# Twelve modulation units of a two-block transformer kernel, moved from GpSimd to TensorE

## What is computed

```python
mod_x = jax.nn.silu(c) @ ada_w[l] + ada_b[l]
sh1, sc1, g1, sh2, sc2, g2 = jnp.split(mod_x[:, None, :], 6, axis=-1)
hx = modulate(rmsnorm(x, norm1_g[l]), sh1, sc1)
...
att_x = latent_attention(qx, jnp.concatenate([kx, kc], axis=1), jnp.concatenate([vx, vc], axis=1))
y_x = merge_branches(fourier_mix(fx), att_x, gx, w_fourier[l], w_mla_o[l], b_gate[l], w_out[l])
x = x + g1 * y_x
h2 = modulate(rmsnorm(x, norm2_g[l]), sh2, sc2)
x = x + g2 * sq_relu_mlp(h2, w_up[l], w_down[l])
```

## Time and profile before

| | |
|---|---|
| median of 3 runs | 2260.36 us (2259.75 to 2266.12) |
| profiled execution | 2260.59 us |
| its span, first to last instruction | 2258.6 us |
| busy: PE, DVE, ACT, POOL | 2176.6, 888.0, 840.9, 880.4 us |
| mean granted TensorE clock | 0.987 |

### The profile page before, as it was taken

The page is one execution under the profiler, slowest core; times in us unless marked ns, Lnnn a source line. Parts: engine busy times, 40 slices in busy tenths (PEclk is TensorE's granted clock), DMA queues, the critical chain, the costliest instruction groups (busy, mean ns, idle before and its releaser), DMA issues.

```text
span 2258.6 us, 28704 instructions
## 1 busy us (share of the span) xinstructions
PE 2176.6 (96%) x11528; PEld 1807.7 (80%) x11528; DVE 888.0 (39%) x1391; ACT 840.9 (37%) x1263; POOL 880.4 (39%) x640
## 2 busy tenths in 40 slices
PE   6999999989999989999999999999999999999998
PEld 3776678868888867989888888787888988888887
DVE  2357955441211246585666210505144243222102
ACT  3456542232322335253543423636233443223212
POOL 0334964434445434031221344041354624444441
PEclk9999989999999999999999999999999999999998
DMA  6411334423232233020211122222233412233221
GB/s 227 161 56 57 114 122 131 156 71 104 97 94 93 94 114 98 20 75 19 94 38 38 56 94 94 76 75 75 75 112 93 150 38 94 93 105 99 93 93 56
DMA packets 179969, 205.89 MB, mean 91 GB/s; under 512 B 3365, under 2 KB 170769, under 8 KB 179473
## 3 DMA queue, kind: packets, MB, share of 16 engines
q1 hardware_dynamic: 176912, 195.17, 26.7%
q10 hardware_dynamic: 2944, 9.15, 1.1%
HBM read 198.01 MB, written 6.29 MB: 90 GB/s over the span
## 4 chain that ended last, share of the span: by engine, by line
PE 81%; POOL 6%; DVE 4%; ACT 2%; issue 1%; DMA 0%; ACTq 0%; DVEq 0%; SPq 0%; POOLq 0%
PE ps L2092 21%; PE ps L2094 21%; PE ps L2093 21%; PE ps L2192 3%; POOL w_lo L692 2%; PE ps L2623 2%; POOL raw L709 2%; PE ps L2636 2%; POOL raw L711 2%; PE ps L2713 2%; PE ps L2730 1%; ACT w_hi L764 1%; PE ps L2139 1%; PE ps L2141 1%; PE ps L2140 1%
## 5 line engine op out<-in xcount | busy, mean ns | idle before, releaser
L692 POOL TENSOR_TENSOR w_lo<-raw,w_hi 128x512 fp32r<-128x512 f32 x586 | 777.2, 1358 | 1313.7 <-ACT w_hi L764 1313.6
L2092 PE MATMUL ps<-h_hi,w_hi 128*128 128x512 f32 x1384 | 558.0, 403 | 14.3 <-DVE h_lo L1427 4.9
L2094 PE MATMUL ps<-h_hi,w_lo 128*128 128x512 f32 x1384 | 542.0, 392 | 0.0
L2093 PE MATMUL ps<-h_lo,w_hi 128*128 128x512 f32 x1384 | 541.3, 391 | 0.0
L764 ACT ACTIVATE w_hi<-raw 128x2048 fp32r<-128x2048 f32 x150 | 285.7, 1904 | 366.2 <-PE ps L2094 359.5
L2092 PEld LDWEIGHTS ps<-h_hi,w_hi 128*128 128x128 f32 x1384 | 261.5, 189 | 75.2 <-issue 10.7
L2094 PEld LDWEIGHTS ps<-h_hi,w_lo 128*128 128x128 f32 x1384 | 261.2, 189 | 56.0
L2093 PEld LDWEIGHTS ps<-h_lo,w_hi 128*128 128x128 f32 x1384 | 262.0, 189 | 52.1 <-issue 1.2
L2092 PE MATMUL ps<-g_hi,w_hi 128*128 128x512 f32 x256 | 99.7, 389 | 0.0
L2094 PE MATMUL ps<-g_hi,w_lo 128*128 128x512 f32 x256 | 99.6, 389 | 0.0
L2093 PE MATMUL ps<-g_lo,w_hi 128*128 128x512 f32 x256 | 99.6, 389 | 0.0
(11 more groups left out here) (422 smaller groups left out, 3815.7 us busy)
## 6 DMA issues: line engine op xcount, KB each, us to landing
raw<-w_in SPq DMA_DIRECT2D x48, 1024.0 KB, 5.2
raw<-w_down SPq DMA_DIRECT2D x27, 1024.0 KB, 5.0
raw<-ada_w SPq DMA_DIRECT2D x24, 1024.0 KB, 5.2
raw<-w_gate_up SPq DMA_DIRECT2D x22, 1024.0 KB, 5.1
raw<-w_up SPq DMA_DIRECT2D x16, 1024.0 KB, 5.4
raw<-w_mkv SPq DMA_DIRECT2D x8, 1024.0 KB, 5.3
raw<-w_out SPq DMA_DIRECT2D x4, 1024.0 KB, 5.3
xT<-bias_band SPq DMA_DIRECT2D x2, 2048.0 KB, 9.8
```

What stands on the lines that cost most here:

```text
L692: ins = nc.gpsimd.tensor_tensor(w_lo[:, split_at[u] % 2, cols], raw[:, u % 2, cols], w_hi[:, split_at[u] % 2, cols].bitcast(F32), ALU.subt ...
L2092: T.matmul(out_, wh, hi, start=start, stop=False, skip_group_check=True)
L2093: T.matmul(out_, wh, lo, start=False, stop=False, skip_group_check=True)
L2094: return T.matmul(out_, wl, hi, start=False, stop=stop, skip_group_check=True)
```

## The change

GpSimd's `modulate` and the two batches in the attention go. The 12 units are multiplied on TensorE, one ahead of the transposes of each even item from 2 to 24 (`ROWS_AT`): the row tiles k = 0 to 3 go to the four column groups of 32 (PSUM partitions 0, 32, 64 and 96), k = 4 to 7 are added to them, with `silu_wide`, 32 columns for each k of which only the first isn't zero. The products lie in the free half of bank 5, so ScalarE's copy of that item takes 1024 columns instead of 768 and brings them into `probT1`. Behind the scores of item 2a + 6 (`PICKED_AT`) TensorE multiplies both halves of unit a's copy by the constant `pick` (1 at partitions 0, 32, 64 and 96), two matmuls of one column, and VectorE adds `ada_b` between its maximum and the scaling of it. VectorE fills `silu_wide` behind item 0. The loads keep their order; a slot is free when the rows are multiplied (`ada_mm`) and not when GpSimd is done. The batch of four in the MLP stays.

The diff, without the list of semaphore names, the value of `pick` and one raised count:

```diff
 CONST_AT, CONST_N = {}, 0
-for _name, _cols in [("ident", P), ("ones", P), ("tri", P), ("incl", P)]:
+for _name, _cols in [("ident", P), ("ones", P), ("tri", P), ("incl", P), ("pick", 1)]:
...
     prob1 = r("prob1", [P, 2, S + C])
-    probT1 = r("probT1", [P, 2, S + C])
-    ada_sum = r("ada_sum", [P, 8, 256])
+    probT1 = r("probT1", [P, 2, S + C + 256])
+    silu_wide = r("silu_wide", [P, KT, 32])
+    ada_sum = r.over("ada_sum", [P, 4, 256], BASE + 92 * 1024)
...
     BY_VECTOR = [12, 13, 14, 15]
-    BY_POOL = [a for a in range(16) if a not in BY_VECTOR]
-    BATCH = [range(0, 10), range(10, 12), range(12, 16)]
+    ROWS_AT = {2 * a + 2: a for a in range(12)}
+    PICKED_AT = {2 * a + 6: a for a in range(12)}
...
-        if a in BATCH[1]:
-            return tmp2[:, :, :].rearrange("p a (b c) -> p (a b) c", c=256)[:, a - 10, :]
-        if a in (8, 9):
-            return acc[:, (a - 8) * 256:(a - 7) * 256]
-        return ada_sum[:, a % 8, :]
+        return ada_sum[:, a % 4, :]
...
     items += [("mem", h, q) for h in range(HM) for q in range(NT)]
-    ADA_ITEM, ADA_BANK = 27, [6, 6, 5]
+    ADA_BANK = 5
...
                         sp.wait_ge(sem["w_lo_half"], lo_half_count(u - 2))
-                elif u - 2 < first["ada_b"]:
+                elif u - 2 < first["merge1"]:
                     sp.wait_ge(sem["ada_mm"], ada_units.index(u - 2) + 1)
-                elif ada_units.index(u - 2) - 8 in BY_POOL:
-                    sp.wait_ge(sem["ada_by_pool"], BY_POOL.index(ada_units.index(u - 2) - 8) + 1)
...
-            def modulate(a):
-                u, chain = ada_units[8 + a], 3 * BY_POOL.index(a)
-                pool.wait_ge(w_in_slot[u % 2], load_count[u])
-                if a == BY_POOL[0]:
-                    pool.wait_ge(sem["c_silu"], 2)
-                    pool.wait_ge(sem["qk_normed"], 10)
-                    pool.wait_ge(sem["qk_turned"], 8)
-                x = raw[:, u % 2, :].rearrange("p (k c) -> p k c", k=KT)
-                def half(k, dst):
-                    pool.wait_ge(sem["pool_chain"], chain + {4: 1, 2: 2, 1: 3}[k])
-                    return nc.gpsimd.tensor_tensor(dst, x[:, 0:k, :], x[:, k:2 * k, :], ALU.add)
-                nc.gpsimd.tensor_tensor(x, x, over_width(silu_c[:, :, 0], 256), ALU.mult).then_inc(sem["pool_chain"], 1)
-                half(4, x[:, 0:4, :]).then_inc(sem["pool_chain"], 1)
-                half(2, x[:, 0:2, :]).then_inc(sem["pool_chain"], 1)
-                half(1, ada_row_of(a).unsqueeze(1)).then_inc(sem["ada_by_pool"], 1)
...
                 if u == first["ada_b"]:
-                    for a in BY_POOL:
-                        modulate(a)
...
                     at_ = turned_bank(n) * 512
+                    if kind == "one" and n in ROWS_AT:
+                        nk += 256
...
-            def modulation(b):
-                at_, n = 16 + 2 * BATCH[b][0], 2 * len(BATCH[b])
-                dve.wait_ge(sem["ada_batch"], b + 1)
-                V.tensor_tensor(mod[:, at_:at_ + n, 0], ps[:, ADA_BANK[b], 0:n],
-                                vecT[:, VEC_AT["ada_b"] + at_:VEC_AT["ada_b"] + at_ + n],
+            def modulation(at_, n, src):
+                V.tensor_tensor(mod[:, at_:at_ + n, 0], src, vecT[:, VEC_AT["ada_b"] + at_:VEC_AT["ada_b"] + at_ + n],
...
                     src = ps[:, :, :].rearrange("p b c -> p (b c)")[:, score_bank(n) * 512:score_bank(n) * 512 + nk]
-                    link(V.reduce_max(at_stat[:, n % 4, 0:1], src, AX.X))
+                    ins = V.reduce_max(at_stat[:, n % 4, 0:1], src, AX.X)
+                    if kind == "one" and n in PICKED_AT:
+                        modulation(16 + 2 * PICKED_AT[n], 2, ps[:, score_bank(n) + 1, 256:258])
+                    link(ins)
...
                         out_lo(n - 2)
-                    if kind == "one" and n == ADA_ITEM:
-                        modulation(0)
+                    if kind == "one" and n == a:
+                        dve.wait_ge(sem["qk_turned"], 10)
+                        link(V.memset(silu_wide[:, :, :], 0.0))
+                        V.tensor_copy(silu_wide[:, :, 0], silu_c[:, :, 0]).then_inc(sem["set_done"], 1)
...
             attention("one", prob1, QK1 ** -0.5, at_hi, at_lo)
-            modulation(1)
-            dve.wait_ge(sem["ada_mod"], 10)
+            dve.wait_ge(sem["ada_mod"], 20)
...
                 if isinstance(count0, int) and count0 == 0:
-                    modulation(2)
-                    dve.wait_ge(sem["ada_mod"], 11)
+                    dve.wait_ge(sem["ada_batch"], 1)
+                    modulation(40, 8, ps[:, ADA_BANK, 0:8])
+                    dve.wait_ge(sem["ada_mod"], 21)
...
-            def modulation(b):
-                pe.wait_ge(sem["ada_by_pool"], len([a for a in BY_POOL if a < BATCH[b].stop]))
-                pe.wait_ge(sem["ada_by_vector"], len([a for a in BY_VECTOR if a < BATCH[b].stop]))
-                if b < 2:
-                    pe.wait_ge(sem["at_out_lo"], 3)
-                    pe.wait_ge(sem["ada_mod"], 8 + b)
-                for i, a in enumerate(BATCH[b]):
+            def modulation():
+                pe.wait_ge(sem["ada_by_vector"], len(BY_VECTOR))
+                for i, a in enumerate(BY_VECTOR):
                     for j in range(2):
-                        ins = T.matmul(ps[:, ADA_BANK[b], 2 * i + j:2 * i + j + 1], ada_row_of(a)[:, j * P:(j + 1) * P],
+                        ins = T.matmul(ps[:, ADA_BANK, 2 * i + j:2 * i + j + 1], ada_row_of(a)[:, j * P:(j + 1) * P],
...
                         ins = T.matmul(ps[:, bank + 1, 0:C], qT[:, h, tok], kT[:, h, S:S + C], start=True, stop=True)
+                        if n in PICKED_AT:
+                            pe.wait_ge(sem["at_copied"], n - 3)
+                            for j in range(2):
+                                ins = T.matmul(ps[:, bank + 1, C + j:C + j + 1], probT1[:, n % 2, S + C + j * P:S + C + (j + 1) * P],
+                                               const[:, CONST_AT["pick"]:CONST_AT["pick"] + 1], start=True, stop=True)
...
+                def ada_rows_of(n, a):
+                    u = ada_units[8 + a]
+                    if a == 0:
+                        pe.wait_ge(sem["set_done"], 2)
+                    pe.wait_ge(w_in_slot[u % 2], load_count[u])
+                    for k in range(KT):
+                        rows = slice(32 * (k % 4), 32 * (k % 4 + 1))
+                        ins = T.matmul(ps[rows, turned_bank(n) + 1, 256:512], silu_wide[:, k, :],
+                                       raw[:, u % 2, k * 256:(k + 1) * 256], start=k < 4, stop=k >= 4, skip_group_check=True)
+                    ins.then_inc(sem["ada_mm"], 1)
...
                     prob = {"one": prob1, "mem": prob_m}[items[n][0]]
+                    if kind == "one" and n in ROWS_AT:
+                        pe.wait_ge(sem["at_copied"], n)
+                        ada_rows_of(n, ROWS_AT[n])
...
                     turned(n)
-                    if kind == "one" and n == ADA_ITEM:
-                        modulation(0)
...
             attention("one", between=last_turns)
-            modulation(1)
...
             pe.wait_ge(sem["at_out_lo"], 4)
-            pe.wait_ge(sem["ada_mod"], 10)
+            pe.wait_ge(sem["ada_mod"], 20)
...
                 if isinstance(count0, int) and count0 == 0:
-                    modulation(2)
+                    modulation()
...
```

More of the change, by code:

```diff
@@ L68, in shape_constants @@
     cols = {"ident": np.eye(P), "ones": np.ones((P, P)), "tri": i[:, None] <= i[None, :],
-            "incl": i[:, None] >= i[None, :]}
+            "incl": i[:, None] >= i[None, :], "pick": i[:, None] % 32 == 0}
     const = np.concatenate([np.asarray(cols[n], np.float32) for n in CONST_AT], axis=1)
@@ L426, in val @@
         return i * (table[u + stride] - table[u]) + table[u]
-    names = """tile_done w_mm_done last_mm w_lo_half w_lo_done x_out x_back ada_mm ada_by_pool ada_by_vector ada_batch pool_chain in_done at_out table_in at_max b_scores b_neg b_min_done b_exp b_turned b_copied b_values b_evicted b_out_turned b_out_hi b_out_lo set_done bias_in y_copied y_copied2
+    names = """tile_done w_mm_done last_mm w_lo_half w_lo_done x_out x_back ada_mm ada_by_vector ada_batch in_done at_out table_in at_max b_scores b_neg b_min_done b_exp b_turned b_copied b_values b_evicted b_out_turned b_out_hi b_out_lo set_done bias_in y_copied y_copied2
     stored w_hi_done bias_ready act_chain n_acc n_sq n_sum n_std n_t n_hi x_in_done c_in_done bc_rope_done
@@ L2710, in scores @@
                     if N + n == 0:
-                        pe.wait_ge(sem["set_done"], 2)
+                        pe.wait_ge(sem["set_done"], 3)
                     query = odd_query(hh // 2) if hh % 2 else qbT[:, hh // 2, :]
```

## The result

The change makes no difference that matters, and a small one that can be measured: 2266.9 us against 2262.7 us, medians of 20 runs each, taken in turn on one chip. One execution of the kernel after took 6020.1 us and stays out of the ratio. The ratio of the times is 1.0016, 95% interval 1.0009 to 1.0024. The forecast was 2264 us, "the same". The profiled execution took 2268.27 us, its span 2266.4.

The account below looks back on a forecast made before the run. TensorE was taken as the bound at 93% of the attention's pace, with GpSimd costing twice. Savings of 16.8 us and additions of 20.4 gave +3.6 us, 2264 us; own range 2258 to 2269, 8 in 10 2256 to 2278.

Parts of the forecast that it names:

- (a): Start of the attention: the first normalisation falls from 2.12 to 0.62 us; -0.7 us taken, between 0 and -1.5.
- (b): Items 1 to 27 of the attention: 13 pairs go from 5.96 to about 5.6 us, -4.7 us.
- (c): Transposes of item 27 to those of item 28: without the stop 3.56 us instead of 14.24, -10.7 us.
- (d): Tail: no slow normalisation ahead of item 29 (about -0.5 us), over_channels no longer waits for the second batch (-0.2 us).
- rival 5: Tail and copies: the tail's low clock stays away and the wide copies hide, -1.3 - 2.5, time 2260; no chance given.
- (e): Row products of 12 units on TensorE: four column groups run at once, 1.03 us a unit, 12.4 us more.
- (f): Picks on TensorE: 12 x 2 matmuls of one column, 0.46 us a unit, 5.5 us more.
- (g): ScalarE's copy of twelve items grows from 768 to 1024 columns: TensorE waits 0.21 us in each, 2.5 us more.
- 1: Row instructions: only two groups overlap, 1.87 us a unit instead of 1.03, +10.1 us, time 2274; chance 0.15.
- 2: Row instructions: no overlap across four groups, 3.7 us a unit, +32 us, time 2296; chance 0.04.
- 4: Attention: TensorE isn't the bound, rows and picks fall into its gaps, -14.3 us, time 2246; chance 0.05.
- 3: Chain of copy, exponentials, scores: another wait, 0.5 us more a pair, +6 us, time 2270; chance 0.06.

Follow-up runs that it names:

- Experiment 1: The changed kernel without row products, picks and wide copy, VectorE copying ada_b instead of adding, loads kept: 2244.49 us, ratio to before 0.9921.
- the split kernel before: The kernel before with GpSimd's multiplication of 2048 columns split in four instructions of 512: 2273.40 us in one execution.
- the second trace of before: The kernel before, unchanged, run once more on another chip for a second trace: 2263.77 us, one execution.
- the split mixture: The mixture with silu_wide filled by GpSimd behind its second unit and GpSimd's multiplication in four instructions: 2261.14 us, ratio to before 0.9994.
- experiment 5: The kernel before with its first batch of turned sums deferred behind the attention, beside the second: 2268.33 us, ratio to before 1.0032.
- Experiment 2: The changed kernel with all eight row products of a unit in one column group: 2297.35 us, ratio to before 1.0154.
- experiment 3: The changed kernel with rows at odd items 3 to 25 and picks at 7 to 29: 2262.14 us, ratio to before 1.0002.
- the mixture: Against the kernel before: GpSimd keeps units 0 to 9, nearly each sum turned singly, units 10 and 11 on TensorE: 2258.78 us, ratio 0.9979.

## Why the prediction was right, and where it was not

The total was forecast at +3.6 us and measured at +3.6. That agreement is luck in part: in the attention, which is all that the sum was about, it should have been +3.6 and was +0.5 to +0.9. The other 3 us lie outside it, where the sum had nothing. Point by point:

- **What bounds the kernel**: right. Experiment 1 leaves TensorE's own 5.61 us a pair; shorter waits of VectorE alone (the split kernel before) bring the same 5.61 in most pairs; both parts of GpSimd's price, through L1578 and through the stop, were separated.
- **(a) start**: -0.7 forecast, 11.36 to 10.65 measured, -0.71; against the second trace of before it is -0.36.
- **(b) items 1 to 27**: -4.7 forecast; 77.44 to 72.84 in experiment 1, -4.6 (-5.4 against the second trace).
- **(c) the stop**: -10.7 forecast, 14.24 to 3.60 measured, -10.64.
- **(d) the tail**: -0.7 forecast, 14.43 to 12.67 measured, -1.76. This is the term that the sum had too small, by 1.06 us, and what it lacked is the clock. The earlier trace rows shows 0.83 for 310 to 320 us, and I put its end in rival 5 instead of the sum. The last values alone fall from 2.83 to 1.53 us, by 1.3. Of my own two parts, the 0.5 for item 29 came: from the transposes of item 28 to the last values it takes 9.46 us instead of 9.95. The 0.2 for the second batch did not, since over_channels now waits 1.68 us for VectorE's `at_lo`. Nor did the second batch bring the clock down. It fell at 311.1 us, ahead of the last values and of that batch (314.56), 10.2 us after it had come back from the stop:

```profile
300.90:311.10 10.20, 7.17 (x70) 5.27 (x66) 6.32 (x11) 6.05 (x9) 5.03 (x4) 1.00 0.52 165
311.10:314.60 3.50, 2.80 (x25) 2.47 (x25) 0.00 (x0) 2.44 (x2) 3.48 (x3) 0.51 0.36 142
```

The kernel after has the same waits there (0.99 and 1.56 us) without a fall. All four traces in which the clock had fallen and come back earlier in the attention (both of before, the split kernel before, the split mixture) show a second fall in the tail; of the other nine only the deferred batch has a low clock there, the one long stretch of experiment 5. So the second fall went with the first, but what ties them together is not shown.
- **(e) rows**: 1.03 us a unit forecast, 1.00 measured. Taking full concurrency from the two-group row was right. Experiment 2 measures the rest: 3.57 in one group, against 3.7 forecast.
- **(f) picks**: 0.46 forecast, 0.43 to 0.44 measured.
- **(g) the wide copy**: 0.21 forecast, 0.17 measured by experiment 3.
- **The pair**: with all of them 5.6 + 1.03 + 0.46 + 0.21 = 7.30 forecast, 7.16 measured, 0.14 less in each of eleven pairs, 1.5 us. 0.10 of it are the three terms' own errors; the rest is that beside 1.00, 0.43 and 0.17 the old work takes 5.56 us, and not 5.6. With the tail that makes up the 2.7 us by which the attention came out under the forecast.
- **(h), (i)**: right. VectorE stays hidden at 621 ns a normalisation, and TensorE never waits for a load in this stretch.
- **Rivals**: 1 and 2 fell to experiment 2, 4 to the pair of 7.16 us, in which TensorE waits for nothing but those 0.17. 3 has not come: ScalarE's delay is the 0.17. 5 came by half, its clock and not its copies.
- **What the sum did not have**: any way for code outside the attention to take another time. Its scatter between traces, 8.6 us, is larger than the whole effect, and it goes with the clock.

## What to carry to other kernels

Work that goes from a helper that stops the bounding engine to that engine itself pays only by the difference: here a stop of 10.6 us and some 7 us of smaller things went for 18.6 us of new matmuls. Before moving all of it, ask which part the helper finishes in time, and move only the rest; the mixture was 4.7 us faster than before, where the full move was 3.6 slower. Put the added work behind the item whose releasing chain has slack (two lines, 2.0 us), and don't collect narrow matmuls behind a wait. By fours between wide ones they cost 0.11 us an instruction. Collected behind a wait, with the clock mostly at its lower level, they cost 0.19 (7.71 us for 40 in the earlier trace rows) to 0.23 (10.9 for 48 in experiment 5). It is the clock that makes the difference: 16 collected at the full clock took 1.84 us in the earlier trace rows, 0.115 each.

## What was not expected of the hardware

- **Column groups**: 16 instructions of 256 columns in four groups took 1.00 us, in one group 3.57. I had only two groups in the trace of before to argue from.
- **Whole-instruction exclusion**: a VectorE tensor_scalar of 0.62 us took 3.85 beside one GpSimd instruction of 3.61, since it ended 0.4 us after that one's end. With GpSimd's multiplication cut in four, the mean fell from 1634 to 1195 ns, but the four took 4.0 to 4.7 us where one took 3.6 to 4.0.
- **The clock after a wait and narrow matmuls**: TensorE's clock was at the lower level for 10.2 us in the stop of the kernel before, for 20.5 in that of the split one, and for 23.9 around the deferred batch. In the split mixture it fell during the 4.5 us wait for a load, with only one unit's picks ahead of it, for 6.8 us. In after's attention, where picks stand between wide matmuls and no wait is over 1.7 us, it did not fall. Waits of that size are no proof against it: before fell a second time behind waits of 0.99 and 1.56.
- **Its price outside the stretch that one looks at**: between two executions of the same code, ahead of the first scores, 10.2 and 23.9 us at the lower clock went with 198.8 and 204.2 us.
